# Prompt attention in a hybrid decoder step: turned weights are made, copied and multiplied one item later

## What is computed

```python
logits = einsum(q, k) * HEAD_DIM ** -0.5
logits = where(valid, logits, -inf)
p = softmax(logits, axis=-1)
o = einsum(p, v)
```

## Time and profile before

| | us |
|---|---|
| median of 3 runs (1151.5 to 1154.43) | 1152.57 |
| the profiled execution, its time | 1146.7 |
| its span, first to last instruction | 1144.9 |
| TensorE busy in the span | 949.7 |
| VectorE, ScalarE, GpSimd busy | 421.1, 274.7, 165.3 |
| the stage `prompt` | 210.8 to 314.3 |

### The profile page before, as it was taken

How to read it: one execution, slowest core, us unless ns; L and a number is a source line. 1 busy time by engine, 2 the same in 40 slices (tenths; PEclk the granted TensorE clock), 3 DMA queues, 4 the chain that set the end, 5 groups by cost and what they waited for, 6 DMA issues and landing times. The chain is left out here.

```text
span 1144.9 us, 14542 instructions
## 1 busy us (share of the span) xinstructions
PE 949.7 (83%) x5829; PEld 555.3 (49%) x5829; DVE 421.1 (37%) x916; ACT 274.7 (24%) x497; POOL 165.3 (14%) x187
## 2 busy tenths in 40 slices
PE   6999999787789999775789999999659987776740
PEld 4544444455565666321579999844523332222210
DVE  3213798556447595112053232111441111010106
ACT  4112211355535777410100000011201100000003
POOL 1100000122012334333400000000011110101012
PEclk9999999899979999888889999999769999999975
DMA  8222020122346997999853642096469999999946
GB/s 268 93 74 73 30 84 19 53 61 93 111 167 222 359 337 226 399 404 411 287 130 84 229 150 58 1 308 217 137 213 374 369 369 366 362 371 368 365 152 229
DMA packets 139265, 246.83 MB, mean 216 GB/s; under 512 B 12432, under 2 KB 104704, under 8 KB 130880
## 3 DMA queue, kind: packets, MB, share of 16 engines
q1 hardware_dynamic: 116944, 142.64, 37.2%
q0 software_dynamic: 21488, 101.05, 23.9%
q10 hardware_dynamic: 768, 2.23, 0.5%
HBM read 238.50 MB, written 15.77 MB: 222 GB/s over the span
## 5 line engine op out<-in xcount | busy, mean ns | idle before, releaser
L683 PE MATMUL bank<-ring,hT 128*128 128x512 f32 (+1 forms) x384 | 160.3, 572 | 0.0
L683 PEld LDWEIGHTS bank<-ring,hT 128*128 128x128 f32 x384 | 71.7, 191 | 79.1 <-issue 69.8
L2026 PE MATMUL bank<-early,obT 128*64 128x512 f32 x352 | 84.0, 626 | 22.1 <-DMA early<-in_w_e_up 20.7
L1293 ACT COPY kT_s<-bank 128x1024 f32<-128x1024 f32 (+1 forms) x90 | 85.6, 996 | 51.6 <-PE bank L1077 51.4
L1077 PEld LDWEIGHTS bank<-consts,ring 128*128 128x128 f32 x704 | 77.5, 142 | 40.5 <-ACT kT_s L1293 34.3
L1077 PE MATMUL bank<-consts,ring 128*128 128x128 f32 x704 | 89.4, 280 | 3.2 <-PEq L227 2.1
L2220 DVE TENSOR_TENSOR uT<-uT,bank 128x256 f32<-128x256 f32 x16 | 6.7, 421 | 206.3 <-ACT uT L2078 206.3
L1566 PE MATMUL bank<-hT_hi,gate_w_hi 128*128 128x272 f32 x224 | 65.9, 294 | 0.0
L2026 PEld LDWEIGHTS bank<-early,obT 128*64 128x64 f32 x352 | 27.7, 143 | 76.6 <-issue 53.9
L1566 PE MATMUL bank<-hT_hi,gate_w_lo 128*128 128x272 f32 x224 | 64.6, 289 | 0.0
L1566 PE MATMUL bank<-hT_lo,gate_w_hi 128*128 128x272 f32 x224 | 64.5, 288 | 0.0
(11 more groups left out here) (367 smaller groups left out, 1429.1 us busy)
## 6 DMA issues: line engine op xcount, KB each, us to landing
early<-in_w_e_gate SPq DMA_DIRECT2D x44, 512.0 KB, 8.9
early<-in_w_e_up SPq DMA_DIRECT2D x44, 512.0 KB, 9.4
early<-in_w_e_down SPq DMA_DIRECT2D x22, 1024.0 KB, 11.4
ring<-in_w_in SPq DMA_DIRECT2D x5, 2048.0 KB, 8.3
w_o<-in_w_e_gate SPq DMA_DIRECT2D x20, 512.0 KB, 8.7
w_o<-in_w_e_up SPq DMA_DIRECT2D x20, 512.0 KB, 9.4
uT<-in_w_e_down SPq DMA_DIRECT2D x10, 1024.0 KB, 11.0
gate_w<-in_w_in SPq DMA_DIRECT2D x14, 512.0 KB, 5.2
```

What stands on the lines that cost most here:

```text
L683: last = nc.tensor.matmul(bank[:, n % 4, 0:WID[g]], s.hT[:, k, t * P:(t + 1) * P], w[:, gi % 2, k, 0:WID[g]], start=(k == 0), stop=(k == K ...
L1293: nc.scalar.copy(kT[:, n % 2, u, :], bank[:, u, :]).then_inc(kT_kept, 1)
L2026: last = nc.tensor.matmul(bank[half(u), 2, :], xT[:, slot % 2, k, half(u)], gate_up_at(s, slot)[:, u, k, :], start=(k == 0), stop=(k == KD ...
```

## The change

On every engine of the stage the loop gets one more turn, and `turn`, `keep_turned`, `keep_second`, `weigh` and the four steps at a group's end are done one turn later than before, relative to `scores`, `tops` and `exps`. In a turn of the loop TensorE does `scores(m)`, `turn(m - 2)`, `weigh(m - 3)`. Buffers, semaphores and what each step waits for stay as they are.

```diff
@@ tensor
-            for m in range(n + 2):
+            for m in range(n + 3):
                 if m < n:
                     scores(m)
-                if 1 <= m < n + 1:
-                    turn(m - 1)
-                if m >= 2:
-                    if (m - 1) % PAIRS == 0:
-                        spread((m - 1) // PAIRS - 1)
-                    weigh(m - 2)
+                if 2 <= m < n + 2:
+                    turn(m - 2)
+                if m >= 3:
+                    if (m - 3) % PAIRS == PAIRS - 1:
+                        spread((m - 3) // PAIRS)
+                    weigh(m - 3)
@@ scalar
-            for m in range(n + 2):
+            for m in range(n + 3):
                 if m < n:
                     exps(m)
-                if 1 <= m < n + 1:
-                    keep_turned(m - 1)
-                if m >= 2 and (m - 1) % PAIRS == 0:
-                    keep_wide((m - 1) // PAIRS - 1)
+                if 2 <= m < n + 2:
+                    keep_turned(m - 2)
+                if m >= 3 and (m - 3) % PAIRS == PAIRS - 1:
+                    keep_wide((m - 3) // PAIRS)
@@ vector
-            for m in range(n + 2):
+            for m in range(n + 3):
                 if m < n:
                     tops(m)
-                if 1 <= m < n + 1 and ITEMS[m - 1][1] == "b":
-                    keep_second(m - 1)
-                if m >= 2 and m % PAIRS == 0:
-                    inverse(m // PAIRS - 1)
-                if m >= 2 and (m - 1) % PAIRS == 0:
-                    normalise((m - 1) // PAIRS - 1)
+                if 2 <= m < n + 2 and ITEMS[m - 2][1] == "b":
+                    keep_second(m - 2)
+                if m >= 2 and (m - 2) % PAIRS == PAIRS - 1:
+                    inverse((m - 2) // PAIRS)
+                if m >= 3 and (m - 3) % PAIRS == PAIRS - 1:
+                    normalise((m - 3) // PAIRS)
```

## The result

| | before | changed |
|---|---|---|
| median, us | 1151.50 (13 runs, 1143.1 to 1154.6) | 1158.09 (13 runs, 1154.0 to 1160.4) |
| the profiled execution, us | 1146.7 | 1157.07 |
| its span, us | 1144.9 | 1155.2 |

The ratio is 1.0058, with a 95% interval of 1.0041 to 1.0074. The change makes the kernel slower by 6.6 us; the forecast was no difference, 1153.0 us in a range up to 1157.0. The result lies outside.

What follows compares the result with a forecast made beforehand. Prompt attention was taken as bound by a chain between engines, 5.71 us per pair of items, unchanged. Start -1.03, end +0.97, VectorE's second copies +0.5 and clock 0 gave +0.4 on 1152.57: 1153.0 us, range 1149.8 to 1157.0.

Steps and rivals of the forecast that it cites:

- The step on the copy: Prompt attention: ScalarE's copy of the turned weights, not the exponentials, ends the transposes' wait; they start 0.1 us behind it.
- the start: Loop start: scores(2) no longer stand behind the first transposes and can start earlier; minus 1.03 us.
- the steady state: Inside the loop: the chain of two items stays 5.71 us per pair after the change; term 0.
- the clock: TensorE's half-clock stretches, 1.62 us each: the same number as before, term 0, with plus or minus one as bounds.
- The first rival: Transposes really wait for their own item's exponentials, so the change saves 21 us, giving 1131.5 us; chance 0.05.
- the remark that with banks 4 and 5 shared by both items: PSUM banks: a longer distance is worth nothing while both items' transposes share them; only a second pair would be.
- the same seven terms with the same sizes: Chain from scores(m) through maximum, exponentials, copy, turn and weigh to scores(m+2): 5.71 us for a pair, as before.
- VectorE's second copies: VectorE's second-half copies (L930): two instead of one beside branch a's long bias at four b-to-a places; plus 0.5 us.
- The end: Loop end: one more turn, in which turn(31) waits for a further transpose and copy; plus 0.97 us.
- The second rival: TensorE's clock falls more often at group ends, up to 1.62 us each; 1157.9 us with three further stretches; chance 0.09.
- The range: Forecast time 1149.8 to 1157.0 us: bounds of the sum, -1.7 and +3.4, with some 1.5 us of spread.

Runs made afterwards that it cites:

- e3: Changed kernel with ScalarE's copy of the turned weights (item m-2) put ahead of the exponentials of item m; 1134.85 us, ratio 0.9880.
- e7: Changed kernel with ScalarE's copies of the turned weights and of the spread reciprocals both ahead of the exponentials; 1131.86 us, ratio 0.9844.
- e9: Changed kernel with 17 unused 256-column matmuls in the waits before the transposes of the third item of seven groups; 1149.87 us, ratio 1.0003.
- e8: Changed kernel run once more without further edits, for a second trace; 1156.76 us, ratio 1.0063.
- e11: Kernel before the change run once more without edits, for a second trace; 1147.90 us, ratio 0.9993.
- e1: Changed kernel with 2 to 9 unused 512-column matmuls before the transposes of the third item of seven groups; 1166.43 us, ratio 1.0149.
- e10: Kernel before the change with 17 unused 256-column matmuls before the transposes of the third item of seven groups; 1147.48 us, ratio 0.9977.

## Why the prediction was wrong, point by point

The step on the copy held. What failed are three terms of the sum: the start, which had the wrong sign (forecast minus 1.03, measured plus 2.06); the steady state, which was put at 0 also where branch b goes over to a (measured 1.57, where the sum had 0.5 for something else); and the clock, which was put at 0 (about 3 us).

**The copy ends the wait: right.** Every wait of the transposes ends 0.10 us behind a copy, before and after the change, and e3 shows the other side of it. The first rival, that the transposes wait for their own exponentials, is out: it would have given 1131.5 us for the change as it is, and such a time came only when the copy was moved too. What doesn't hold is the remark that with banks 4 and 5 shared by both items only a second pair of banks would make the distance worth anything: e3 and e7 gained 17.1 and 20.6 us in the stage with the same two banks.

**The steady state, 0: right within a group, wrong at passages.** Scores of items 11 and 13, a pair with three blocks, start 5.71 us apart in e9 as they did before. With the short mask the two orders keep their distance within 0.1 us from item 2 to item 26. The sum of "the same seven terms with the same sizes" failed where branch b goes over to a. There the exponentials ahead of a branch b item's copy are now those of a branch a item, whose bias takes 1.23 us instead of 0.43 with four blocks, 0.97 with three, 0.70 with two. That makes 0.80, 0.54 and 0.27, and the trace has 0.80, 0.53 and 0.24: together 1.57 us. I had put 0.5 there for VectorE's second copies, the wrong instruction.

**The start, minus 1.03: wrong in sign, and 3.1 us off.** The scores of item 2 do start earlier. But scores that run ahead end nothing; the stage ends with the last weigh. What counts is when the transposes start, and they start one chain's step later: 2.06 us at full clock. I had followed the chain of scores to its end and assumed that the transposes behind it were the same ones; they are those of one item before.

**The end, plus 0.97: not seen.** From item 30 to item 31 the distance falls by 0.17 us in both pairs of runs (2.80 to 2.62, 2.72 to 2.55). The extra turn was already paid at the start. With the start and the passages this gives 3.5 us for the order, where the sum had 0.4.

**The clock, 0 with one stretch either way: as large a miss as the start.** Of the 6.6 us, 3.1 are left beyond the order's 3.5. The difference of the medians with fillers is 2.4, so by that measure some 4 us went away when the waits were filled. Both figures are estimates with an uncertainty of a few us, but the granted clock of all executions (0.922 against at least 0.926, and 0.928 for both with fillers) goes the same way. By the first trace, the distance grew from 2.06 us before item 14 to 3.43 before item 15, from 3.65 to 4.75 between items 22 and 23, and from 4.75 to 6.81 between items 26 and 29, at 271, 294 and 305 us, where the clock fell. The second rival had this mechanism and its place. That its 1157.9 us, with three further stretches, is so near the 1158.09 measured is luck: it starts from a median of 1152.57 where 13 executions have 1151.50, and it has 4.9 us of clock and 0.4 of order where the runs have about 3 and 3.5. I gave it 0.09 because the later waits are shorter than the one of 2.58 us at which the clock had fallen. That was one trace. After the change the waits before items 14 and 22 are 2.27 and 1.74 us, against 1.98 and 1.53 before, and the clock fell there in both traces of the changed kernel (beginning with item 14 or 15, and with item 22 or 23) and in neither of the kernel before.

**The range** took its upper end from one stretch and left out the likelier way to be slower. Its ends also don't follow from the spread it names: with 1.5 us they would be 1149.4 and 1157.5, and 1149.8 and 1157.0 come from 1.07, the distance from the median to the lowest of the three times. The measured 1158.09 lies outside either.

What stays open is why the clock fell where it did. The changed kernel has longer waits before items 14 and 22 and fell there in both traces, but its other falls move between two executions of the same program, and in e8 the longest wait passed without one. Four traces can't tell how much comes from the length of the waits and how much from the moment at which they fall. Nor do the runs fix the two shares of the loss within less than a few us: in the second pair of traces (e8 and e11) the stages are only 2.6 us apart, less than the 3.5 us of the order: e11 lost 1.6 us to the clock at item 6, where e8 lost nothing.

## What to carry to other kernels

A longer distance between the stages of a loop brought nothing here while the step that frees the shared buffer was queued behind the step that ends last. With the freeing step first on its engine the distance paid: minus 1.2%, and minus 1.6% with the group's copy ahead too, instead of plus 0.6%. The freeing step first without the distance gave minus 0.3%. When an order is shifted by one item, write down which item now stands ahead of which at every change of kind or size, and follow the steps that end the stage, not those that run ahead. When a wait has several releasers, compare its end with the ends of all of them: the name in the list was wrong for most of the time here. And where a loop has gaps on TensorE behind which its clock has been seen to fall, make more falls a rival with a real chance. Filling the gaps with matmuls that compute nothing, in both kernels, is a cheap way to see what the clock costs.

## What the runs showed of the hardware

Filler matmuls without any use made the changed kernel faster, from 1.0058 to 1.0003 of the kernel before; the trace has the granted clock at 1.00 for 88 us with them. One f32 matmul call of the filler (64x128 by 64x512) is two instructions, 0.44 us each in a row of them, as e1 showed (18 in 7.88 us). Between two executions of one program the stretches at the lower clock move: 243, 271, 294, 305 and 315 us in one trace, 272, 294 and 312 us in the other. A wait of 2.80 us left the clock at 1.00 once (e8), and waits of 2.58, 2.27 and 1.74 us had lower clocks right behind them in other executions.

The Trainium skill, page TensorE: Matmul & The Clock Gate, section What's actually happening, states that idle time sends TensorE to 1.2 GHz and busy time brings it back to 2.4. The fillers agree with it: with the waits filled, the granted clock was 1.00 from 221 to 309 us in e9 and from 221 to 311 us in e10.
